# A context's output projection moved behind the experts, and two norms of the latent taken in one round

## The reference, cut to what matters

```python
x = x + gt2 * hier_moe(modulate(rms_norm(x, norm2_g), sh2, sc2), ...)   # latent, block one
x = rms_norm(x, final_norm_g)                                           # end of block one
# block two, layer 0
hx = rmsnorm(x, g_pre[0]) * (1 + scale) + shift
hc = rmsnorm(ctx, g_pre[0]) * (1 + scale_c) + shift_c
yx, yc = mlstm_pool_mixer(hx, hc, ...)          # ends in concat([y_m, y_p]) @ ab_w_out
x = x + gate * rmsnorm(yx, g_post[0])
ctx = ctx + gate_c * rmsnorm(yc, g_post[0])
# layer 1 starts with rmsnorm(ctx, g_pre[1]) and rmsnorm(x, g_pre[1])
```

## Time and profile before

| | us |
|---|---|
| median of 3 runs (lowest, highest) | 1808.93 (1799.91, 1812.79) |
| the profiled execution, its own time | 1805.27 |
| its span on the core | 1803.5 |
| PE busy | 1586.6 (88% of the span) |
| DVE, ACT busy | 488.0, 339.2 |
| mean granted clock of PE | 0.922 |

### The profile page before, as it was taken

The page is one execution under the profiler, slowest core; times in us unless marked ns, Lnnn a source line. Parts: engine busy times, 40 slices in busy tenths (PEclk is TensorE's granted clock), DMA queues, the critical chain, the costliest instruction groups (busy, mean ns, idle before and its releaser), DMA issues.

```text
span 1803.5 us, 21928 instructions
## 1 busy us (share of the span) xinstructions
PE 1586.6 (88%) x9261; PEld 1078.5 (60%) x9261; DVE 488.0 (27%) x1222; ACT 339.2 (19%) x698; POOL 4.1 (0%) x8
## 2 busy tenths in 40 slices
PE   5799949898988878997998999976889999979797
PEld 2555649777877334453455664455676685867566
DVE  2200164541224241122213100024343231020581
ACT  2211230112121111202110001023112122121371
POOL 0000000000000000000000000000000000000000
PEclk9999966799978989998999999986899999989999
DMA  9577750132224989999999999951313313322000
GB/s 346 218 297 280 297 245 1 47 123 113 94 96 170 421 333 370 399 398 419 403 409 410 411 419 405 384 210 36 140 47 140 135 52 140 144 100 103 38 1 24
DMA packets 54304, 397.57 MB, mean 220 GB/s; under 512 B 6360, under 2 KB 13689, under 8 KB 16441
## 3 DMA queue, kind: packets, MB, share of 16 engines
q1 hardware_dynamic: 40384, 341.85, 47.4%
q10 hardware_dynamic: 13240, 52.16, 7.3%
q0 software_dynamic: 576, 2.10, 0.3%
HBM read 389.80 MB, written 6.29 MB: 220 GB/s over the span
## 4 chain that ended last, share of the span: by engine, by line
PE 76%; DMA 8%; DVE 8%; ACT 4%; issue 2%; PEld 1%; SPq 0%; ACTq 0%; PEldq 0%; DVEq 0%
PE bank L660 14%; PE bank L1373 12%; PE bank L1388 8%; PE bank L2300 6%; DMA work<-in_moe_w_up 4%; PE bank L2317 4%; PE bank L1488 3%; PE bank L1493 3%; PE bank L518 2%; PE bank L2286 2%; PE bank L689 2%; PE bank L1095 2%; PE bank L1083 2%; PE bank L840 1%; DMA work<-in_ab_pool_w 1%
## 5 line engine op out<-in xcount | busy, mean ns | idle before, releaser
L660 PE MATMUL bank<-H,ring 128*128 128x256 f32 (+1 forms) x928 | 244.4, 424 | 18.2 <-DVEq L294 8.2
L660 PEld LDWEIGHTS bank<-H,ring 128*128 128x128 f32 x928 | 178.8, 194 | 78.4 <-issue 49.3
L2300 PE MATMUL bank<-ring,work 128*32 128x512 f32 (+1 forms) x768 | 142.8, 656 | 19.2 <-DMA work<-in_moe_w_up 10.4
L1373 PE MATMUL bank<-H,work 128*128 128x256 f32 x512 | 116.7, 387 | 0.3 <-issue 0.3
L1373 PE MATMUL bank<-H,ring 128*128 128x256 f32 x512 | 112.9, 381 | 0.0
L1373 PEld LDWEIGHTS bank<-H,work 128*128 128x128 f32 x512 | 97.7, 193 | 19.6 <-issue 6.4
L1373 PEld LDWEIGHTS bank<-H,ring 128*128 128x128 f32 x512 | 98.1, 192 | 13.6
L2300 PEld LDWEIGHTS bank<-ring,work 128*32 128x32 f32 (+1 forms) x768 | 37.2, 126 | 111.9 <-issue 87.8
L1388 PE MATMUL bank<-work,H 128*128 128x512 f32 x192 | 85.2, 597 | 0.0
L1388 PE MATMUL bank<-ring,H 128*128 128x512 f32 x192 | 83.0, 592 | 0.0
L2317 PE MATMUL bank<-ring,work 128*32 128x512 f32 (+1 forms) x384 | 66.9, 611 | 2.8 <-issue 2.2
(11 more groups left out here) (403 smaller groups left out, 2010.5 us busy)
## 6 DMA issues: line engine op xcount, KB each, us to landing
ring<-in_moe_w_gate SPq DMA_DIRECT2D x48, 1024.0 KB, 11.6
ring<-in_moe_w_up SPq DMA_DIRECT2D x48, 1024.0 KB, 9.6
ring<-in_moe_w_down SPq DMA_DIRECT2D x48, 1024.0 KB, 12.1
work<-in_ab_w_in ACTq DMA_DIRECT2D x28, 1024.0 KB, 10.2
ring<-in_ab_w_in SPq DMA_DIRECT2D x14, 2048.0 KB, 7.5
ring<-in_ada_w SPq DMA_DIRECT2D x12, 2048.0 KB, 7.6
ring<-in_w_in SPq DMA_DIRECT2D x12, 2048.0 KB, 7.5
ring<-in_w_mod SPq DMA_DIRECT2D x12, 2048.0 KB, 7.7
```

What stands on the lines that cost most here:

```text
L660: mm = nc.tensor.matmul(bank[i % NB][:, 0:n], weight(c, k, j * P, (j + 1) * P), rhs(k), start=(k == 0), stop=(k == kt - 1))
L1373: mm = nc.tensor.matmul(b[:, j * T:(j + 1) * T], w_k(m, n, k, at, at + P), H[:, k, m.s], start=(k == 0), stop=(k == DT - 1), skip_group_ch ...
L2300: mm = nc.tensor.matmul(bank[b][rows, :], gath[:, k, rows], half_slot[(load_at[n + half] + e) % NHALF][:, (k % 4) * 512:(k % 4 + 1) * 512] ...
```

## The change

1. `body_*` end behind PG: `out_*`, and the context's norms behind it, are no longer in the experts' stage. `FILL_FOUR` falls from 16 to 12 steps a pass, `FILL_TWO` rises from 2 to 3. The order of the passes stays (the list is only written once).
2. `last1_*`: the output projection of the context runs among the chain of the latent's norms, four steps at a time. The two norms of the latent (final norm, norm ahead of layer 0) are one round: ACT squares X and X times the final norm's weights, PE sums both, DVE and ACT derive the second inverse root from the first (`fused`), PE spreads both, and DVE writes H for layer 0 and the normed X. H's latent half holds the context's y_m, so DVE waits for the last matmul of the projection.
3. `mix_*` no longer starts with a norm. The context's norm behind the projection (`post`) and the one ahead of layer 1 (`after`) stand inside it: around O and Z, and around Q and K of the second pair of heads.
4. SP waits for the end of the last pass for all three ring slots, and for the stores of all passes' rows, before it loads the latent's weights.

```diff
-        FILL_FOUR, FILL_TWO = (2, 2, 2, 2, 2, 2, 2, 1, 1), (0, 0, 0, 1, 0, 1, 0, 0, 0)
+        FILL_FOUR, FILL_TWO = (1, 1, 1, 1, 2, 2, 1, 2, 1), (0, 0, 1, 1, 0, 0, 0, 1, 0)
...
             for c in range(2):
                 yield from tiles_pe(pe, m, PG[c])
-            yield from out_pe(pe, m)
-            yield from norm_steps_pe(pe, m)
-            yield from norm_steps_pe(pe, m)
...
         def last1_pe(pe):
+            out = out_pe(pe, mixers[0])
             for j in range(DT):
...
                 mm.then_inc(accT_mm, 1)
-            norm_pe(pe, H, T)
+            take(out, 4)
+            u = norm_use["pe"]
+            pe.wait_ge(accT_out, DT)
+            for i, src in enumerate((sq_x, sq_g)):
...
+            take(out, 4)
+            norm_use["pe"] += 2
+            for i in range(2):
+                pe.wait_ge(rinv_done, u + i + 1)
...
+                take(out, 4)
+            finish(out)
...
         def last1_dve(dve, chain):
...
+            finish(out_dve(dve, mixers[0]))
+            dve.wait_ge(a_mm, turns["dve_a"])
+            dve.wait_ge(rstd_mm, STD_BEFORE[u + 1])
...
         def mix_pe(pe):
...
-            finish(norm_steps_pe(pe, m))
+            post = norm_steps_pe(pe, mixers[0])
+            after = norm_steps_pe(pe, mixers[0])
             gates_pe(pe, m)
...
+            next(post)
             finish(rows_pe(pe, m, O[0]))
+            finish(post)
             finish(rows_pe(pe, m, Z[0]))
...
             finish(tiles_pe(pe, m, Q[1]))
+            next(after)
             finish(tiles_pe(pe, m, K[1]))
+            finish(after)
...
             moe_sync(sp)
...
+            for i in range(2):
+                sp.wait_ge(rows_stored[i], 16 * (NPASS // 2))
             for j in range(len(second)):
                 load_chunk(sp, AT_SECOND + j)
```

More of the change, by code:

```diff
@@ L37 @@
 CAP = CAP_WIDE
+PASSES = [(N_WIDE + 4 * i, 4) for i in range((NX - N_WIDE) // 4)] + [(2 * i, 2) for i in range(N_WIDE // 2)]
+NPASS = len(PASSES)
 MH, MD = 4, 256
@@ L110, in shape_constants @@
     c["tri"] = np.triu(np.ones((P, P)))
[L111 to L114, removed]
     by_lane = np.zeros(NX)
-    by_lane[lanes] = lane_base
+    for p, (first, experts) in enumerate(PASSES):
+        by_lane[first:first + experts] = P * p + np.arange(experts) * (P // experts)
     c["slot_no"] = np.tile(np.concatenate([np.arange(CAP), by_lane]), (P, 1))
@@ L2686, in build, with take @@
         accT_mm, accT_out = sem("accT_mm"), sem("accT_out")
-        x_first = sem("x_first")
+        sq_x = hrows.rearrange("p t d -> p (t d)").rearrange("p (k t) -> p k t", t=T)
+        sq_g = work[:, WORK - 2 * DT * T:WORK - DT * T].rearrange("p (k t) -> p k t", t=T)
+        fused = sem("fused")
+        def take(steps, n):
+            for _ in range(n):
+                next(steps, None)
         def last1_pe(pe):
+            out = out_pe(pe, mixers[0])
             for j in range(DT):
@@ new lines, in last1_act @@
+        def last1_act(act, chain):
+            m = mixers[0]
+            out = out_act(act, m)
+            for k in range(DT):
+                act.wait_ge(accT_out, k + 1)
+                nc.scalar.activation(sq_x[:, k, :], X[:, k, 0:T], ACT.Square).then_inc(sq_ready, 1)
+            for k in range(DT):
+                nc.scalar.activation(sq_g[:, k, :], X[:, k, 0:T], ACT.Square, scale=vec("fng", k, k + 1)).then_inc(sq_ready, 1)
+            take(out, 4)
+            u = norm_use["act"]
+            norm_use["act"] += 2
+            act.wait_ge(sumsq_done, STD_BEFORE[u])
+            nc.scalar.activation(rstd[:, u % 2, 0:64], bank[0][:, 0:64], ACT.Sqrt, bias=epsc[:], scale=1.0 / D).then_inc(std_done, 1)
+            take(out, 4)
+            act.wait_ge(fused, 1)
+            nc.scalar.activation(rstd[:, (u + 1) % 2, 0:64], rstd[:, (u + 1) % 2, 0:64], ACT.Sqrt, bias=epsc[:]).then_inc(std_done, 1)
+            finish(out)
+            modulate_act(act, mod2, 0, (0,))
@@ L2715, in both @@
+            for k in range(DT):
+                V.scalar_tensor_tensor(out=X[:, k, 0:T], in0=X[:, k, 0:T], scalar=vec("fng", k, k + 1), in1=bank[2][:, 0:T], op0=ALU.mult, op1=ALU.mult)
         def both(a, b):
@@ L2751, in mix_act @@
             act.dma_start(m.pool_inv, d["pool_inv"]).then_inc(pool_in, 16)
[L2752 removed]
+            post = post_act(act, mixers[0])
+            after = next_act(act, mixers[0], x_new, 0, mod2, 24)
             gate_in_act(act, m)
@@ L2774, in mix_dve @@
             wide_from.update(dve_d=turns["dve_d"])
-            finish(next_dve(dve, chain, m, vec("gpre", 0, 8), mod2, 8))
+            post = post_dve2(dve, chain, mixers[0])
+            after = next_dve(dve, chain, mixers[0], vec("gpre", 8, 16), mod2, 32)
             ones_dve(m)
@@ L2792, in mix_dve @@
             finish(heads_dve(dve, m, 0))
-            for c in range(4):
-                conv_dve(dve, chain, m, 4 + c)
+            for c in (4, 5):
+                conv_dve(dve, chain, m, c)
+            next(after)
+            for c in (6, 7):
+                conv_dve(dve, chain, m, c)
+            finish(after)
             a_seen(2)
```

65 lines of the change are left out of this document (41 added, 24 removed).

## The result

The changed kernel takes 1852.58 us (median of 4 runs, 1847.27 to 1860.26); the kernel before, on the same chip, 1804.77 (4 runs, 1799.91 to 1812.79). The ratio is 1.0264, with a 95% interval of 1.0206 to 1.0321: slower by 48 us. The forecast was 1826 with a range up to 1850. The direction was right, the size was not, and the result lies 2.6 us above the range.

A forecast was written before the change was run, and what follows sets the result against it. DMA, fuller than a nearly full PE, was taken to bound the experts' stage, PE alone what follows. Fours -38.6, twos +3.5, behind the passes +48.6, mix +7.0 gave +20.5 on 1805.3: forecast 1826 us, range 1802 to 1850.

The forecast's parts named there:

- Fours: Experts' stage, 483.8 us before: DMA-bound, shrinking to 445.2 us, 38.6 saved (25.1 to 51.3).
- the middle: DMA rate in the fours: 409 GB/s, between today's 397 and the highest long stretch's 421.
- Rival B: Fours: PE's cold restarts free slots late, DMA stays at 397 GB/s, 1839 us (1854 at 385 GB/s); chance 0.30.
- Twos: Experts' stage, 134 us before: PE sets this part with 138 us, +3.5.
- Behind the passes: From the last fill to the first Q tile: 66.35 us becomes 114.9, +48.6.
- a wait of 4: Behind the passes: PE waits 4 us (0 to 17) for the weights of PG's second tile.
- Rival C: Behind the passes: PG's or the first output weights land at 23.7, not 10.2, 13.5 more, 1839 us; chance 0.08.
- The expert rows: Behind PG: last silu 0.6, scaling and adding the rows 3.6, barrier until PE runs 1.6, together 5.8 us.
- last1: Behind the passes on PE: transposes 3.4, 16 output steps 55.3, sums 2.5, spreads 2.2, together 63.4 us.
- H, X and the barrier: Behind the last output matmul: DVE writes H and X uncovered, 6.5 us, then the barrier, 1.6.
- the gates: End of the stretch behind the passes: 5.9 us, at half clock as before.
- Mix: Q to the output projection: the two norms' added sums, spreads and waits all show, +7.0 us (2.5 to 12).

The follow-up runs named there:

- experiment 5: Changed kernel, its twelve fills of a four placed (2,2,2,1,0,2,1,1,1) instead of (1,1,1,1,2,2,1,2,1): 1834.32 us, ratio 1.0187.
- experiment 10: Changed kernel with the even fills of experiment 5 and the early ring loads of experiment 8: 1813.34 us, ratio 1.005.
- 14 steps (6): Changed kernel with fills of 14 and 2, so the whole body in the passes and only the output projection behind them: 1827.83 us, ratio 1.0141.
- experiment 9: Changed kernel, whole body in the passes, four fills (2,2,2,1,0,2,2,2,1), SP's latent loads behind the gather of the rows: 1826.18 us, ratio 1.0128.
- Experiment 7: Kernel before, only its sixteen fills of a four moved, (2,2,2,1,1,2,2,2,2) instead of (2,2,2,2,2,2,2,1,1): 1811.44 us, ratio 1.0055.
- experiment 4: Changed kernel with both fill tables zero, the body running at the end, only the fours to be read: 2005.44 us.
- experiment 1: Changed kernel, SP also waiting for PG's second pair of weights before loading the latent's 2 MB tiles: 1845.44 us, ratio 1.0236.
- 3: Kernel before with only the two fill tables of the changed kernel: 1859.19 us, ratio 1.0291.
- experiment 8: Changed kernel with part 4 undone, SP loading the latent's tiles early without waiting for the row stores: 1839.54 us, ratio 1.0192.
- experiment 2: Kernel before with only the latent's two norms fused into one round, nothing of the projection moved: 1804.27 us, ratio 0.9993.

## Why the prediction was right and wrong

**Fours: the step that failed.** "I take the middle, 409 GB/s". The bytes were right (459.3 us at 398 GB/s are 182.8 MB, forecast 182.1), the rate wasn't. I put it between today's and the highest row and called less fill the reason that it rises. Less fill on average doesn't raise it; what decides is how long PE goes between two used steps. I had named that interval in the same sentence, with its three fills, and still took the middle. Counted now, in body steps between two used steps of a four:

| kernel | behind three halves | up to down | in down | behind down | GB/s |
|---|---|---|---|---|---|
| before | 2, 2, 2 | 4 | 2 | 4 | 397 |
| changed | 1, 1, 1 | 3 | 2 | 4 | 398 |
| even (5, 10) | 2, 2, 2 | 1 | 2 | 3 | 415, 416 |
| 14 steps (6) | 2, 2, 2 | 2 | 2 | 4 | 415 |
| 14 steps (9) | 2, 2, 2 | 1 | 2 | 5 | 405 |
| before, moved (7) | 2, 2, 2 | 2 | 2 | 6 | 396 |
| no fills (4) | 0, 0, 0 | 0 | 0 | 0 | 417 |

The change took three of its four steps a pass from intervals that had room and one from the one that hadn't. Today's rate of 397 gave 25.1 us saved in the forecast's own sum; 24.5 were. Of the miss in the fours, 14.1 us, placement explains all: experiment 5 gets 438.0, below the 445.2 forecast. The counts alone don't rank every row: the kernel before and the changed one move the same with four and three steps from up to down. The least disturbed comparison is experiment 9 against 6, where one step of fourteen moves and 10 GB/s go.

**Rival B had the right number for the wrong reason.** It too said 397 GB/s, by way of PE's cold restarts. In experiment 4 the granted clock is 0.67 to 0.79 all the way, and DMA moves 417; in experiment 5 it is 0.91 as in the changed kernel, and DMA moves 415. The Trainium skill (TensorE: Matmul & The Clock Gate, Part 1: The HAM clock gate) describes the throttled state after idle, and the 6.14 us of a step behind a wait agree; but where DMA is the bound that costs nothing here. As to the 358 GB/s that the forecast cited from the Trainium skill (DMA: Bandwidth & Descriptors, Bandwidth): the note under that section's measured sizes gives them for a core whose neighbour streams too, and the measurement is 425 GB/s for a core alone, which the forecast left out. Runs on one core here agree with the second figure: 417 over 386.7 us, 422 at the height.

**Twos.** +1.0 against +3.5; PE was busy 130.65 of 135.0, against 138 worked out. PE sets this part, as said. Two terms were off and partly cancel: the four passes' matmuls took 99.1 us and not 107.2, since the last has no next one to gather for and the transposes take 0.6, not 1.4; the body's steps took 34.0 and not 31.1.

**Behind the passes: the second step that failed.** "SP's two new waits cost nothing, and take those loads out of the row stores' way". The second half of that holds: POOL's first gather, which waits for the store, comes 3.5 us behind the store's issue (1156.34 to 1159.85) instead of 11. The first is wrong by 14 us: I looked at when the latent's weights are due, 90 us later, and not at what they push aside when they start late. The waits put 6.3 MB, in the largest packets, into the moment in which PG's second pair is fetched. I had priced that pair at a wait of 4, by its median landing, although the extremes were in the same row; it was 14.5, and 2.5 more in the tile that follows it at a lower granted clock (16.48 against 13.97). Experiment 5, with the same waits, has the same hole (14.33). Rival C had the mechanism and nearly the size (13.5 more), and I gave it 0.08. Experiments 1, 3 and 8 show the cause from three sides: ring loads later, ring loads as in the kernel before, and part 4 alone undone.

**The other terms of that stretch** leave 1.5 us. The expert rows, priced at 5.8 from PG's end to the transposes, took 8.87: ACT first issues two loads (1.4), and the barrier comes 3.3 behind DVE's sum and not 1.6. last1 was 62.9 against 63.4. H, X and the barrier took 6.5 against 8.1, the gates 6.4 against 5.9. With the waits taken back the whole stretch is 113.6 in experiment 10, with a wait for PG of 1.50; the same sum gives 110.9 without any and 114.9 with the 4.

**Mix** came out at +7.0, as forecast. Each of its new rows is there: one set of sums hidden but for its own PE time, one behind ACT's squares, two spreads. They make 6.6 us with the wait:

```profile
1396.43 1.10 PE L1209 MATMUL bank<-H,ones 128*32 128x64 f32 x64
...
1411.30 1.00 PE L1219 MATMUL bank<-rstd,ident 128*128 128x64 f32 x8
...
1448.79 2.37 PE L1209 MATMUL bank<-H,ones 128*32 128x64 f32 x64 [1.08 <-ACT H L1653]
...
1465.01 1.00 PE L1219 MATMUL bank<-rstd,ident 128*128 128x64 f32 x8
```

**The sum.** The forecast's central claim is shown: the idle time around the norms isn't enough to pay for work that DMA mostly hid. What the rearranged norms do give, mix included, was 17.7 us by its terms and is 19 (experiment 8 against 3). Put the measured 416 GB/s and no wait for PG into its terms and they give -46.1 + 3.5 + 44.6 + 7.0 = +9.0; experiment 10 measured +7.6 between the spans and +12 between the medians. No version here beats the kernel before: experiment 2 isn't told apart from it, 7 and 10 are half a per cent slower. What stays open is why the kernel before holds 397 GB/s with sixteen steps a four: whether a placement without a long interval exists that reaches 415, or PE, busy 435 of 484 us, is the bound by then. Experiment 7 moved the long interval and didn't settle it.

## What to carry to other kernels

Where a transfer is bound by slots, count the longest time between two slots coming free, with every piece of work and every wait in it, and compare it with what is still on order when it begins, here one to two loads of 10 us; the average work per load didn't tell 398 from 415 GB/s. A wait that delays a prefetch isn't priced by when the prefetch is needed, but by what is being loaded at the moment to which it is moved. A loading's median landing time is no price for a load in a crowd: look at what else goes out within 10 us of it, and in what packets.

## What the runs showed of the hardware

- The DMA engines move 415 to 417 GB/s into one core over 387 to 447 us, with single stretches at 422. The same stage moved 397 in the kernel before.
- DMA's rate didn't suffer from a low clock of PE: 417 GB/s at a granted clock of 0.79 (experiment 4), the highest over a whole stretch here.
- Three queues shared the DMA engines by turns of a packet, not by bytes and not in the order of issue: 335, 318 and 394 packets, but 4.70, 2.35 and 1.48 MB in 20.2 us. The Trainium skill (DMA: Bandwidth & Descriptors, Queues, rings and completion order) says that an engine takes its queues in turn, a packet at a time, and the trace agrees. By equal thirds of the bytes PG's 2.1 MB would have been in after 15 us (an estimate from the 422). By the 28% that ACT's queue got it is 18 us, and that queue had moved 0.25 MB beyond PG's by then; the second half landed 21.0 us after its issue. The last gather, issued at 1163.71, ahead of PG's weights, landed 27.1 us later, behind them.
- Behind a wait of 4.13 us PE's next tile took 17.11 us instead of 13.97, at a granted clock of 0.53 in its first 6.5 us (experiment 1). Behind one of 1.68 us it took 14.05, at a clock of 1.00 (experiment 8).
